# Narrow logits turned round, the first mixer reordered, X in halves, and filler products at four waits

## The reference

```python
h = rmsnorm(x, mix_norm[l]); z = h @ w_in[l]                       # first block, 1 layer
q, k, v, f_logit, gate_in, rec_in = jnp.split(z, split_points, axis=-1)
att = forgetting_attention(q, k, v, log_f)                          # 8 heads of 64, causal, with decay
rec = rg_lru(causal_depthwise_conv(rec_in, conv_w, conv_b), w_a, b_a, w_x, b_x, lam)
x = x + concat([att, rec * gelu(gate_in)]) @ w_out[l]
y = hierarchical_moe(rmsnorm(x, ffn_norm[l]), ...)                  # 4 groups of 8 experts, width 256
x = rmsnorm(x + y, final_norm)
for layer in range(4):                                              # second block
    x = x + 0.5 * rms_norm(swiglu_ffn(rms_norm(x, g[0]), ...), g[1])
    x = x + rms_norm(mixer(rms_norm(x, g[2])), g[3])                # mLSTM, RWKV-7, retention, mLSTM
    x = x + 0.5 * rms_norm(swiglu_ffn(rms_norm(x, g[4]), ...), g[5])
```

## Time and profile before

| | |
|---|---|
| median of three runs | 2735.07 us |
| the profiled execution | 2733.12 us, its span 2731.2 us |
| PE busy | 2675.1 us, 98% of the span |
| DVE, ACT, POOL busy | 1812.3, 1413.5, 141.8 us |
| mean granted TensorE clock | 0.991 |
| read from HBM | 488.38 MB, 179 GB/s |

### The profile page before, as it was taken

The page is one execution under the profiler, slowest core; times in us unless marked ns, Lnnn a source line. Parts: engine busy times, 40 slices in busy tenths (PEclk is TensorE's granted clock), DMA queues, the critical chain, the costliest instruction groups (busy, mean ns, idle before and its releaser), DMA issues.

```text
span 2731.2 us, 47800 instructions
## 1 busy us (share of the span) xinstructions
PE 2675.1 (98%) x19686; PEld 2413.6 (88%) x19686; DVE 1812.3 (66%) x2213; ACT 1413.5 (52%) x1872; POOL 141.8 (5%) x227
## 2 busy tenths in 40 slices
PE   7999999999999999999999999999999999999999
PEld 7899999888998888879998888889988888899887
DVE  5555688766566666679757667666566676656665
ACT  5544577655555455458325445454345454455544
POOL 3000000100000000000301000000000000000000
PEclk9989999999999999999999999999999999999999
DMA  7165799665535555544304556556445555553553
GB/s 210 47 209 173 260 358 357 231 201 194 154 131 193 193 185 193 185 138 139 111 4 142 196 186 202 185 170 198 150 170 193 187 191 188 196 153 130 196 186 123
DMA packets 371308, 491.97 MB, mean 180 GB/s; under 512 B 12320, under 2 KB 331392, under 8 KB 371136
## 3 DMA queue, kind: packets, MB, share of 16 engines
q1 hardware_dynamic: 367984, 479.51, 53.1%
q0 software_dynamic: 2576, 7.97, 1.0%
q10 hardware_dynamic: 576, 1.98, 0.2%
HBM read 488.38 MB, written 1.05 MB: 179 GB/s over the span
## 4 chain that ended last, share of the span: by engine, by line
PE 93%; DVE 3%; ACT 2%; issue 1%; POOL 1%; DMA 0%; ACTq 0%; DVEq 0%; POOLq 0%
PE bank L367 21%; PE bank L366 11%; PE bank L346 9%; PE bank L348 9%; PE bank L347 9%; PE acc L346 8%; PE acc L348 8%; PE acc L347 8%; PE bank L3152 1%; PE bank L3129 1%; PE bank L3140 1%; DVE w_lo L316 1%; PE bank L1679 0%; PE acc L711 0%; DVE X L579 0%
## 5 line engine op out<-in xcount | busy, mean ns | idle before, releaser
L316 DVE TENSOR_TENSOR w_lo<-raw,w_hi 128x2048 fp32r<-128x2048 f32 x349 | 798.7, 2291 | 411.7 <-ACT w_hi L311 411.3
L311 ACT ACTIVATE w_hi<-raw 128x2048 fp32r<-128x2048 f32 x349 | 667.0, 1913 | 256.8 <-PE acc L348 222.5
L367 PE MATMUL bank<-act_both,w_hi 128*128 128x512 f32 x2560 | 654.8, 392 | 1.5 <-DVE w_lo L316 1.5
L367 PEld LDWEIGHTS bank<-act_both,w_hi 128*128 128x128 f32 x2560 | 465.2, 189 | 84.8 <-DVE w_lo L316 1.9
L366 PEld LDWEIGHTS bank<-act_both,w_lo 128*128 128x128 f32 x2560 | 349.2, 190 | 25.0
L346 PE MATMUL acc<-w_hi,mix_hi 128*128 128x512 f32 x920 | 361.5, 393 | 4.0 <-ACT att_probs L1350 2.2
L348 PE MATMUL acc<-w_hi,mix_lo 128*128 128x512 f32 x920 | 359.1, 390 | 0.0
L347 PE MATMUL acc<-w_lo,mix_hi 128*128 128x512 f32 x920 | 358.6, 390 | 0.0
L366 PE MATMUL bank<-act_both,w_lo 128*128 128x256 f32 x2560 | 357.0, 282 | 0.0
L904 ACT ACTIVATE scratch<-bank 128x256 f32<-128x256 f32 x320 | 121.7, 383 | 426.8 <-PE bank L367 420.3
L346 PE MATMUL bank<-act_both,w_hi 128*128 128x256 f32 x1032 | 296.3, 287 | 6.0 <-DVE act_both L3455 2.6
(11 more groups left out here) (557 smaller groups left out, 3977.2 us busy)
## 6 DMA issues: line engine op xcount, KB each, us to landing
raw<-in_ffn_w_gu SPq DMA_DIRECT2D x176, 1024.0 KB, 5.1
raw<-in_ffn_w_down SPq DMA_DIRECT2D x88, 1024.0 KB, 4.9
raw<-in_ml_w_in SPq DMA_DIRECT2D x24, 1024.0 KB, 5.3
raw<-in_rt_w_in SPq DMA_DIRECT2D x24, 1024.0 KB, 5.2
raw<-in_w_up SPq DMA_DIRECT2D x20, 1024.0 KB, 8.0
raw<-in_w_gate SPq DMA_DIRECT2D x19, 1024.0 KB, 7.5
raw<-in_w_down SPq DMA_DIRECT2D x18, 1024.0 KB, 7.1
moe_raw<-in_w_down SPq DMA_DIRECT2D x14, 1024.0 KB, 7.1
```

Source lines behind the costliest of these rows:

```text
L311: act.activation(w_hi[0:rows, slot, 0:size], raw[0:rows, slot, 0:size], ACT.Copy).then_inc(hi_made, 1)
L316: dve.tensor_tensor(w_lo[0:rows, slot, 0:size], raw[0:rows, slot, 0:size], w_hi[0:rows, slot, 0:size].bitcast(F32), ALU.subtract).then_inc ...
L367: return pe.matmul(bank[b][:, :], w_hi[:, slot, w], act_both[:, k, :], start=k == 0, stop=k == KT - 1)
```

## The change

It joins four edits.

1. Narrow logits. The 8 or 36 weight columns are now the stationary operand and 256 (mLSTM) or 128 (MoE) tokens move; the result lies with columns on partitions, so ACT copies it to SBUF (`rows`) and PE turns it back (`pe_narrow_turn`). In the mLSTM the panel `v` 2 stands between `rows` and the turned `if`, and ACT does the tanh, exp and logarithm behind that panel. `den` and `num` are interleaved head by head.
2. First mixer. The gates come right behind the gate projection, the square root and the scan before the scores; the split behind `q` 1 and that of the narrow weights move behind the exponentials of all eight heads.
3. Opening. X comes in two DMAs, the second weight panel waits on SP for the first of them, the rest of the constants moves from ACT's queue to SP's; both tiles are turned before any projection; five warming products (float32, 512 columns, of a zeroed tile) stand on PE while X is on its way.
4. Fillers. `pe_filler` issues float32 products of 128x512 whose result nobody reads: 3 and 2 in `pe_cross`, 1 and 3 around `count`, 2 at the head of `pe_final`.

```diff
+        def pe_narrow(pe, n, a, cols, tok, wait=None):
 
             for k in range(KT):
                 if wait:
                     wait(k)
-                tok = slice(t * P, t * P + P)
-                last = split_product(pe, bank[n % BANKS][:, t * cols:t * cols + cols], act_hi[:, k, tok],
-                                     act_lo[:, k, tok], narrow_hi[:, k, a:a + cols], narrow_lo[:, k, a:a + cols],
-                                     k == 0, k == KT - 1)
+                last = split_product(pe, bank[n % BANKS][0:cols, tok], narrow_hi[:, k, a:a + cols], narrow_lo[:, k, a:a + cols],
+                                     act_hi[:, k, tok], act_lo[:, k, tok], k == 0, k == KT - 1)
             return last
 
...
+        def pe_narrow_turn(pe, n, rows, cols):
+
             for t in range(TT):
-                last = pe_narrow_half(pe, n, t, a, cols)
-            last.then_inc(tensor_done, 1)
+                last = pe.transpose(bank[n % BANKS][:, t * cols:t * cols + cols], rows[0:cols, t * P:t * P + P],
+                                    ident[0:cols, 0:cols])
+            return last
...
+        def act_load(act, c, g):
...
+            act.wait_ge(x_loaded[0], 16)
+            act.activation(scratch[:, 0, 0:512], X[:, 0, 0:512], ACT.Square, scale=1.0 / 32.0,
+                           accum_out=ssq[:, 4:5]).then_inc(x_summed_act, 1)
+            act.wait_ge(ident_loaded, 16)
+            act.wait_ge(mix_ready, 1)
+            spread(0)
+            act_split(act, 0, 1, None)
+            spread(1)
+            high(0)
+            act_split(act, 1, 1, None)
+            high(1)
+            act_split(act, 2, 1, None)
+            c.crossed()
...
+        def dve_load(dve, c, g):
...
+            dve.tensor_copy(vecs[:, 0:MIX_ROWS], acc[3][:, 0:MIX_ROWS]).then_inc(mix_ready, 1)
+            dve.wait_ge(x_loaded[0], 16)
+            dve_x_sum(dve, 0)
+            dve.wait_ge(x_loaded[1], 16)
+            dve_x_sum(dve, 1)
+            dve.wait_ge(x_summed_act, 1)
+            dve.scalar_tensor_tensor(scratch[:, 1, 0:512], X[:, 1, 0:512], 1.0 / D, X[:, 1, 0:512], ALU.mult, ALU.mult,
+                                     accum_out=ssq[:, 6:7]).then_inc(x_summed_act, 1)
+            dve.wait_ge(mix_ready, 1)
+            dve_split(dve, 0, 0)
+            lower(0)
+            lower(1)
+            dve_split(dve, 1, 1)
+            dve_split(dve, 2, 2)
...
+            if c.end == "load":
+                b = acc[2 * t + k // 2] if k < 4 else bank[1 if t else k // 2]
+                at = k % (4 if t and k > 3 else 2)
...
+        def pe_filler(pe, dst, times):
+
+            for _ in range(times):
+                pe.matmul(dst[:, :], ident, con[:, 0:512], start=True, stop=True)
+
         def pe_cross(pe, c, low=True):
+            pe_result_free(pe, c.n)
             for t in range(TT):
                 pe_turn(pe, c, t, low)
+                pe_filler(pe, bank[c.n % BANKS], 3 - t)
             c.crossed()
...
+        def pe_load(pe, c):
...
+            first, second = ((w_hi[:, q % RING, :], w_lo[:, q % RING, :]) for q in (p, p + 1))
+            for t in range(TT):
+                pe.wait_ge(diag_ready, t + 1)
+                for k in range(KT):
+                    last = pe.matmul(turn_place(c, t, k), X[:, t, k * P:k * P + P], diag[:, t, :], start=True, stop=True)
+                    if k % 2:
+                        last.then_inc(turned, 1)
+            dst = bank[n % BANKS][:, 0:PW]
+            for k in range(KT):
+                pe.wait_ge(hi_made, p + 1)
+                pe.wait_ge(norm_hi, k // 2 + 1)
+                pe.matmul(dst, act_hi[:, k, 0:P], first[0][:, k * PW:k * PW + PW], start=k == 0, stop=False)
+            pe.wait_ge(lo_made, p + 1)
+            for k in range(KT):
+                pe.matmul(dst, act_hi[:, k, 0:P], first[1][:, k * PW:k * PW + PW], start=False, stop=False)
+            for k in range(KT):
+                pe.wait_ge(normed, k // 2 + 1)
+                pe.matmul(dst, act_lo[:, k, 0:P], first[0][:, k * PW:k * PW + PW], start=False, stop=k == KT - 1)
+            c.lows += 1
+            pe_half(pe, n % BANKS, first, 1, after_norm(pe, c, 1)).then_inc(tensor_done, 1)
+            pe.wait_ge(lo_made, p + 2)
+            pe_half(pe, (n + 1) % BANKS, second, 0)
+            pe_half(pe, (n + 1) % BANKS, second, 1).then_inc(tensor_done, 1)
+            c.lows -= 1
...
-            act.dma_start(X[:, :, :], d["x"][0].rearrange("(t p) c -> p t c", p=P)).then_inc(x_loaded, 16)
-            act.dma_start(con[:, P:], consts[:, P:]).then_inc(consts_loaded, 16)
+            for t in range(TT):
+                act.dma_start(X[:, t, :], d["x"][0, t * P:t * P + P, :]).then_inc(x_loaded[t], 16)
...
+            dve.memset(gated[:, 1, :], 0.0).then_inc(warmer_ready, 1)
...
         def pe_setup(pe):
+            def warmer(n):
+                for _ in range(n):
+                    pe.matmul(acc[2][:, :], gated[:, 1, 0:P], gated[:, 1, :], start=True, stop=True)
+
+            pe.wait_ge(warmer_ready, 1)
+            warmer(2)
             pe.wait_ge(ident_loaded, 16)
...
                       stop=True).then_inc(mix_turned, 1)
             pe.wait_ge(mix_ready, 1)
+            warmer(3)
```

```diff
                 at = IN_A[part] + half * PW
+                if j == 1:
+                    sp.wait_ge(x_loaded[0], 16)
                 if j == RING:
+                    sp.dma_start(con[:, P:], consts[:, P:]).then_inc(consts_loaded, 16)
                     sp.wait_ge(cleared, 3)
                     for dst, src in vec_loads[1:]:
...
-            ahead("gate", 1)
-            act.wait_ge(narrow_loaded, 16 * len(narrow_loads))
-            act.activation(narrow_hi[:, :, :], narrow[:, :, :], ACT.Copy).then_inc(narrow_high, 1)
-            act.wait_ge(narrow_low, 1)
             for j in range(4):
                 gates(j)
-            projected("q", 0)
-            ahead("q", 0)
+            ahead("gate", 1)
             att_dve.wait(act, "lam_scaled")
             for j in range(4):
                 powers(j)
+            projected("q", 0)
+            ahead("q", 0)
+            att_dve.wait(act, "square")
+            att_act.done(act.activation(lru_t[:, :, :], lru_t[:, :, :], ACT.Sqrt), "sqrt")
             projected("k", 0)
             ahead("k", 0)
             projected("q", 1)
             for h in range(4):
                 exps(h)
-            ahead("q", 1)
-            att_dve.wait(act, "square")
-            att_act.done(act.activation(lru_t[:, :, :], lru_t[:, :, :], ACT.Sqrt), "sqrt")
+            lru_high(0)
+            lru_high(1)
             projected("k", 1)
             for h in range(4):
                 turned_copy(h)
-            exps(4)
-            exps(5)
-            lru_high(0)
-            lru_high(1)
+            for h in range(4, 8):
+                exps(h)
             high(0)
             high(1)
-            exps(6)
-            exps(7)
             turned_copy(4)
             turned_copy(5)
+            ahead("q", 1)
             ahead("k", 1)
             high(2)
...
@@ -1528,6 +1602,15 @@
             att_dve.done(dve.scalar_tensor_tensor(lru_t[:, :, :], lru_r[:, :, :], 1.0, lru_t[:, :, :], ALU.add, ALU.mult),
                          "square")
             ahead("q", 0)
+            att_act.wait(dve, "sqrt")
+            own(dve.tensor_tensor(lru_i[:, :, :], lru_i[:, :, :], lru_t[:, :, :], ALU.mult))
+            for j in range(4):
+                last = dve.tensor_tensor_scan(lru_r[:, j, :], lru_a[:, j, :], lru_i[:, j, :], 0.0, ALU.mult, ALU.add)
+            att_dve.done(last, "u")
+            att_dve.wait(dve, "u")
+            for j in range(2):
+                wait_evacuated(dve, N["gate", j])
+                lru_out(j)
             ahead("k", 0)
...
-                last = pe_narrow_half(pe, N["logits",], t, 0, 36, after_norm(pe, c, t))
+                    pe_result_free(pe, N["rows",])
+                last = pe_narrow(pe, N["rows",], 0, 36, slice(t * P, t * P + P), after_norm(pe, c, t))
                 c.lows -= 1
             last.then_inc(tensor_done, 1)
+            pe_result_free(pe, N["logits",])
+            wait_evacuated(pe, N["rows",])
+            pe_narrow_turn(pe, N["logits",], logit_rows, 36).then_inc(tensor_done, 1)
...
+            pe_filler(pe, acc[0], 1)
...
+            pe_filler(pe, acc[0], 3)
...
+            pe_result_free(pe, n)
+            pe_filler(pe, bank[n % BANKS], 2)
...
-            pe_narrow(pe, N["if",], 36 + 8 * r, 8)
+            pe_result_free(pe, N["rows",])
+            done(pe_narrow(pe, N["rows",], 36 + 8 * r, 8, slice(0, T)))
             project("v", 2)
+            pe_result_free(pe, N["if",])
+            wait_evacuated(pe, N["rows",])
+            done(pe_narrow_turn(pe, N["if",], ml_gT, 8))
```

More of the change, by code:

```diff
@@ L533, in act_cross @@
                 high(0)
-            if between:
-                between(1)
-            elif not last and c.end != "summed":
+            if not last and c.end != "summed":
```

(28 more changed lines are left out.)

118 lines of the change are left out of this document (58 added, 60 removed).

## The result

| | before | after |
|---|---|---|
| median, us | 2734.89 (2730.14 to 2736.38, 4 runs) | 2703.6 (2703.19 to 2704.11, 4 runs) |
| profiled execution; its span | 2733.12; 2731.2 | 2704.11; 2702.0 |
| PE busy | 2675.1 | 2667.1 |
| mean granted clock | 0.991 | 0.999 |

The ratio is 0.9881, with a 95% interval of 0.987 to 0.9893: 31.3 us less, where 26 were forecast (2709; range 2702 to 2722). Of the 31.3 the two profiled executions show 29.0; the rest is that each stands off its median, by 1.8 and 0.5 us.

A forecast was written before the change was run, and what follows sets the result against it. TensorE was taken to bound the kernel, 2675.1 us busy in a span of 2731.2. The terms -9.8 - 7.7 - 4.3 - 3.2 - 1.2 - 0.5 sum to -26.7 on 2733.12, 2706.4; median 2708.4, said as 2709, range 2702 to 2722.

The forecast's parts named there:

- the table's forecasts: Gains by stage, us: opening 4.3, first mixer 7.7, router 3.2, out of the MoE 0.5, mLSTM 9.8, RWKV crossing 1.2.
- the prediction's own terms, 741.4 and 3.16 us: mLSTM: ACT's copy and split end at 741.4; then tanh, exp, logarithm at 0.2 each and two table loads of 1.28.
- The zero for `den` and `num`: mLSTM: `den` ends 2.6 us later, squares and scales by 0.8, but nothing of it reaches PE: 0.
- The sign that I had named against it: Opening: a wait of PE on a weight panel before 60 us would make the prediction wrong.
- The queue rival: Opening: PE waits for panel 4 or 5 as small loads fill the engines; costs the 4.3: 2713, chance 0.10.
- the slower one: Opening: small rows on SP stall four times 6.57 us, and the opening's 4.3 is lost: 2740, chance 0.04.
- the bounds 0.06 and 0.22: Router, us per fp32r product with 128 moving columns: half the 256-column price from below, plain float32 from above.
- fillers: hidden at full clock, 1.7 us over at half: Router: fillers of 0.86 and 2.6 us fit waits of 1.4 and 2.9 at full clock; 1.7 over at half.
- the stretch loses some 2.0: Router: behind the logits, at clock 0.73, `count` gains 1.0, DVE bounds the gathers' end; some 2.0 us go.
- The rival with float32's price: Router: narrow fp32r products cost what float32 does, so its term becomes +2.1: 2714, chance 0.24.
- The rival of the fast rule: Router: the Trainium skill's N/2.4 + 2.5 ns, 56 for 128 columns, gives -5.5: 2706, chance 0.10.
- The clock's rival: Whole kernel: narrow-array products or fillers keep the clock no better; 2 x 2.7 + 1.4 + 1.5 come back: 2717, chance 0.07.

The follow-up runs named there:

- `den` first: The changed kernel with den ahead of all four num again in the two mLSTM layers: 2706.57 us, ratio 0.9898.
- the fillers alone: The kernel before with only the filler products added (RWKV crossing, around count, out of the MoE): 2733.34 us, ratio 0.9993.

## Why the prediction was right, and where it was not

Of the 5.4 us between 2709 and 2703.6 only 2.3 are the stages': the sum gave 2706.4 for the profiled execution, which took 2704.11. I then set the median 2.0 above that, as it had been before; it came 0.5 below. Rounding gave the last 0.6. Against the table's forecasts the stages gained -0.6, +0.9, +2.6, +0.9, +0.6 and -1.8 us more, in its order. That only the router's miss is left in the sum is luck: the others cancel.

**mLSTM: right.** 24 products take 2.80 us (2.9 forecast) and the 96 behind them run at 1.00. The groups by form of the changed kernel (the mean counts what a record overlaps with the next; the products start 0.117 us apart in the first group):

```profile
L347 PE MATMUL bank<-act_both,narrow_hi 128*8 128x256 f32 x16 | 4.4, 277 | 0.0
L347 PE MATMUL bank<-act_both,narrow_hi 128*36 128x128 f32 x16 | 3.4, 235 | 1.0 <-DVE act_both L578 0.9
```

ACT's logarithm ends 0.42 us before PE's `b` begins (0.3 forecast; the prediction's own terms, 741.4 and 3.16 us, make 744.6 and so 0.5):

```profile
724.93 0.21 ACT L2523 ACTIVATE ml_nl<-ml_e 128x8 f32<-128x8 f32 x1
```

The zero for `den` and `num` holds between the two traces: in the kernel before, with the twelve one-column products in a row, the clock is 1.00 behind them in both layers. But it was argued incompletely. I looked only for who waits for `den`, not at the clock. In two other kernels with that order, `den` first and the fillers alone, the clock falls behind them for 3.4 us in layer 3 and costs some 1.7.

**First mixer: right**, 8.6 for 7.7, wait by wait: 2.0 at the gates, 2.0 of the 2.3 at `att_kz` (0.3 stays; 0.4 was forecast), 3.2 at `out_rows` (2.6, though the two waits named for it, 2.2 and 0.6, make 2.8; 0.3 of the 3.2 is clock before 104.16), and 1.37 (25.96 - 24.59) for the clock (1.4). That the split of the narrow weights had a part in the wait at the gates isn't borne out: put back early, it makes none.

**Opening: right in size (3.7 for 4.3), half wrong in its working.** The first half of X lands later than the rate taken from the earlier trace rows gave:

```profile
1.81 5.65 DMA X<-in_x
```

At 7.46, not 6.7, so the first turn begins at 10.43, not 9.5. The five warming products, on which I made full clock depend, matter little: 2.6 us at the turns, 1.2 at the second panel, 0.7 in the median, since DVE holds the stage. The sign that I had named against it, a wait of PE on a weight panel before 60 us, did appear, but what it waits for is DVE's split of the second panel, which the prediction had ending at 21.3, and not a load:

```profile
21.84 0.39 PE L347 MATMUL bank<-w_hi,act_both 128*128 128x256 f32 x1 [1.06 <-DVE w_lo L317]
```

The queue rival and the slower one are out: no wait of PE on a load is seen before 60 us, and the rows of SP's queue show no stall like the 6.57 us of before.

```profile
8.59 1.67 SPq L1240 DMA_DIRECT2D con<-shape_constants  x1
10.30 0.39 SPq L1243 DMA_DIRECT2D setup_rows<-in_ffn_norm  x1
```

**Router: the sign right, the size wrong, 5.8 for 3.2.** Two terms failed. The price of a product with 128 moving columns: 24 take 2.0 to 2.1 us, 0.087 each, between the bounds 0.06 and 0.22 and below the 0.12 that I took: 1.7 us for both halves. The other is "fillers: hidden at full clock, 1.7 us over at half", in a sum that had "the stretch loses some 2.0". I priced the fillers for the time they take and gave them nothing for the clock. Without them the router takes 2.5 us more (29.30 against 26.84) and the whole kernel 4.7. The 5.8 holds while the clock does: with the same router and the old opening it would be 3.9 (28.74 us). The rival with float32's price is out. The rival of the fast rule, which gave 2706 by a router term of -5.5, comes nearest to the time, but its price of 0.06 was not measured.

**Crossings.** Out of the MoE 1.4 for 0.5: the fillers' 1.7 us delayed the turn but not the products behind it, and the half-clock stretch there is gone. At the RWKV crossing 0.9 for 1.2. The clock's rival (2717) is out as well: 3.4 us at half clock are left of 47.8.

**Not explained.** Within the RWKV mixer, from 1225 to 1378 us, the changed trace gives back 1.5 us of its lead, mostly in steps of some 0.3 inside groups of products that are the same. In ten of the other thirteen traces the steps at `rw_r,rw_k` are absent. What stalls PE there was not tried.

## What to carry to other kernels

Look at the granted clock where PE is busy without a gap: a few microseconds of products that move 1 to 36 columns can cost twice, in themselves and in a half-clock stretch behind. Turn them so that the many tokens move. To interleave what can't be turned helped `den` in one layer of two; a single filler amid the thin products did not help. Fill a wait where the clock is still up when the wait begins, since the fillers behind thin products ran at half clock and outlasted the wait. Ask first whether another engine paces the stretch, for then little of either reaches the end. And before an edit is blamed or praised for 1 to 3 us, set the half-clock stretches of both traces side by side.

## What the hardware showed unexpectedly

- An fp32r product with 128 moving columns and 36 stationary ones takes 0.087 us in a row of 24, against 0.117 with 256 moving and 8 stationary (2.80 / 24): half the moving columns, with more stationary ones, take a quarter less.
- In all fourteen traces the half-clock stretches within the run are 3.4, 6.8, 10.2 or 17.1 us long, with PE busy throughout in several. The same order of instructions lost the clock in one layer and not in the other (`den` first), and such a stretch stands at the end of the 16 thin products of `sum`, or within 1.3 us behind it, in eleven of the thirteen traces that have them. What decides between the two isn't shown.
- Fillers on the kernel before took nothing off the router's time at half clock: two stretches of 6.8 and 10.2 us became one of 17.1.
